# Reordering the rotation sums and the recurrence gates of a one-core, three-layer transformer kernel

## The chip, the core and the metric

The kernel runs on one core of a Trainium2 chip. The metric is the device time of one execution in microseconds (us). The kernel before takes 1228.55 us, the median of three runs (1228.42 to 1229.12).

## The reference

The input is a sequence of 256 tokens of width 1024, in float32. Two layers of a first block and one layer of a second block follow one another. Cut to what matters here:

```python
# first block, layer 1 ("odd"): dilated attention; 3 groups x (q, k, v) x 16 heads of 64
hcat = (rms_norm(x, g) @ w_in).reshape(b, s, 3, 3, 16, 64)
q = apply_rope(hcat[:, :, :, 0], cos, sin)     # x1*c - x2*s | x2*c + x1*s
k = apply_rope(hcat[:, :, :, 1], cos, sin)
v = hcat[:, :, :, 2]
x = x + dilated_attention(q, k, v) @ w_o
x = x + square(relu(rms_norm(x) @ w1)) @ w2    # both layers end in this MLP

# second block
proj = rms_norm(x, g) @ w_in_2                 # 7 parts: xa, ga, qm, km, vm, qx, gate logits
xa = causal_dwconv(xa, conv_w, conv_b)         # 4 taps, 512 channels
r = sigmoid(xa @ w_a + b_a); i = sigmoid(xa @ w_x + b_x)   # per head, 8 heads of 64
log_a = -8 * r * softplus(-lam)
u = sqrt(-expm1(2 * log_a)) * i * xa
h_t = exp(log_a)_t * h_(t-1) + u_t             # recurrence over the tokens
y_a = h * gelu(ga)
# then block attention, cross-attention, three gated branches, a gated MLP with a convolution
```

## The kernel before, in words

Every weight matrix is cut into 192 slabs of up to 1 MB, which the program uses strictly in order. A slab goes through the same steps each time. SyncE (SP) loads it into one of five buffers `raw`. ScalarE (ACT) rounds it to a reduced float format, `whi` (three buffers, `high`, line 1118). VectorE (DVE), or in some stages GpSimd (POOL), subtracts the two to get the rest, `wlo` (five buffers, `low`, line 1558). TensorE (PE) multiplies `whi` and `wlo` with the activations, which are split in the same way into `XH` and `XL`. Three products are added up in PSUM: high by high, high by low, low by high. The code calls the step that makes slab n+2 ready `ahead(n)`.

The order of the work on each engine is written by hand: five functions (`tensor`, `scalar`, `vector`, `gpsimd`, `sync`) issue each engine's instructions in program order, and named events tie them together. An engine that waits for an event holds up all that stands behind it on that engine.

A slab whose products are feature-major is computed by one of two functions. `features` (through `product`, line 536) goes chunk by chunk: high weight, low weight, high weight, so its second matmul already needs `wlo`. `features_low_last` (line 550) first does all 32 matmuls that use `whi`, then the 16 that use `wlo`. Both issue 48 matmuls of 256 columns. `tokens` and `by_tokens` are token-major.

**The odd stage** has the slabs 50 to 85, and i counts them from 0. The first ten (`EARLY`) come before the attention steps start; i = 0 to 5 are q and k slabs, 6 to 8 are v slabs, 9 is again q. A q or k slab is rotated as follows. ACT copies the product from PSUM into `TA` (line 1376), and its queue starts four DMAs that write the halves swapped into `TB` (line 1382). POOL multiplies `TB` by the sine (line 2339; the event `sine`). DVE multiplies the PSUM product by the cosine (line 1939) and later adds `TB` (line 1918, function `rotate`; the event `rotated`). ACT may copy slab k only when slab k-2 has been added. In the first ten slabs `rotate` runs one slab behind: the sum of slab k stands on DVE behind `ahead` of slab k+2 and ahead of that slab's cosine product.

**The in2 stage** has the slabs 122 to 133, and n counts them from 0. DVE scales each product (line 2014) and runs one of four causal convolutions (`conv(0)` to `conv(3)`, lines 2039 and 2043) at n = 1 to 4. On PE, `lru_gate` (line 994) multiplies the convolved chunks 0 to 3 by the small gate matrices; it is issued twice, behind n = 6 and n = 7. Its chunk c waits for `conv(c)`. ACT takes the sigmoid (line 1413), then a tanh (line 1437) at n = 8 and an exponential (line 1442) at n = 9; DVE forms a ratio in two parts (lines 2056 to 2060) at n = 9 and 10; ACT takes a root (line 1446) at n = 11; then comes the recurrence (line 2073) during the first attention steps.

Of the kernel before, what the change touches and what calls it, by code (L numbers as in the profile page):

```python
# [7 lines left out]
ALU = mybir.AluOpType  # L8
# [71 lines left out]
class Tally:  # L80
# [9 lines left out]
    def tell(self, sem, *events, by=1):  # L90
        n = self.count[sem.name] = self.count.get(sem.name, 0) + by
        for event in events:
            if self.rehearsing:
                assert event not in self.value, event
                self.value[event] = sem, n
            assert self.value[event] == (sem, n), event
        return sem, by

    def at(self, event):
        return self.value.get(event, (None, 0)) if self.rehearsing else self.value[event]  # L100
# [117 lines left out]
DILATED = dilated_slabs()  # L218

EARLY = 10  # L220
# [74 lines left out]
def build(nc, A, out):  # L295
    with ExitStack() as ctx:
# [216 lines left out]
        def tensor(pe):  # L513
            once = Once(pe)
# [434 lines left out]
            def odd_slab(i):  # L949
                n, (kind, hb, g, k) = SLAB_ODD + i, DILATED[i]  # L950
                if i == 0:
                    features_by_chunks([n, n + 1], x, lambda: last_rows_back(0))
                    sums("n2", 1, cols=True, dilated=True)
                elif kind == "qk":
                    if i > 1:
                        (features_low_last if i < 6 else features)(n, x)
                elif kind == "v":
                    tokens(n, x)
                else:
                    for t in range(2):  # L960
                        if k == 0:
                            bank(("odd v", hb, g, t))
                        b = ps[bank_of.get(("odd v", hb, g, t), 0)]
                        event = ("product", "odd v", hb, g, t) if k else ("weights", n) if t else None
                        xt = [(h[:, t * P:t * P + P], l[:, t * P:t * P + P], mh, ml) for h, l, mh, ml in x[4 * k:4 * k + 4]]
                        product(b[:, :], xt, w_ready(n, 4, 0, 512), event, first=k == 0, last=k == 1)
                    released[n] = [event]
# [17 lines left out]
            def lru_gate(n):  # L985
                for j in range(2):
                    b = bank(("lru", n, j))
                    once.wait_ge(*at("lruw"))
                    for m in range(2):
                        c = 2 * j + m  # L990
                        once.wait_ge(*at(("conv", c)))
                        for a in range(2):
                            p = slice(64 * a, 64 * a + 64)
                            mm = pe.matmul(b[p, m * S:(m + 1) * S], wab[p, n, c, :], XC[p, c, :], start=True, stop=True)  # L994
                    mm.then_inc(*tell(s_product, ("product", "lru", n, j)))
# [11 lines left out]
            for n in range(12):  # L1007
                if n == 0:
                    features_by_chunks([IN2, IN2 + 1], x, lambda: last_rows_back(1))
                elif n == 1:  # L1010
                    pass
                elif n in (6, 7):
                    by_tokens("in2 values", IN2 + n, n - 6)
                else:
                    (features_low_last if n < 6 else features)(IN2 + n, x)
                if n == 0:
                    sums("n4", 1, cols=True)
                    sums("n5", 0, cols=True)
                if n in (6, 7):
                    lru_gate(n - 6)  # L1020

            def gate(j):
                by_tokens(("gate", j // 2), BLENDS + BLEND.index(("gate", j)), j % 2)
# [81 lines left out]
        def scalar(act):  # L1105
# [301 lines left out]
            def lru_gate(n):  # L1407
                dst, bl = ((AR, "ba"), (UI, "bx"))[n]
                for j in range(2):
                    b = take(("lru", n, j))  # L1410
                    for m in range(2):
                        c = 2 * j + m
                        i = act.activation(dst[:, c, :], b[:, m * S:(m + 1) * S], ACT.Sigmoid, bias=gain(bl, c))
                    i.then_inc(*tell(s_act_out, ("taken", "lru", n, j)))
# [6 lines left out]
            for n in range(12):  # L1421
                if n != 1:
                    ahead(IN2 + n)
                if n == 0:
                    root("n4", 1, cols=True)
                    ahead(IN2 + 1)
                    once.wait_ge(*at("both mean"))
                    act.activation(RS[:, 0, 0:S + 2], RS[:, 0, 0:S + 2], ACT.Sqrt).then_inc(*tell(s_root, "both sqrt"))
                if n == 7:
                    by_tokens("in2 values", lambda t: VB[:, t, :])  # L1430
                if n in (6, 7):
                    lru_gate(n - 6)
                if n == 8:
                    once.wait_ge(*at("rate"))
                    for c in range(4):
                        once.wait_ge(*at(("taken", "lru", 1, 1)))
                        m = act.activation(UM[:, c, :], AR[:, c, :], ACT.Tanh, scale=L[6][:, c:c + 1])
                    m.then_inc(*tell(s_act, "lru tanh"))
                if n == 9:
                    once.wait_ge(*at("lru tanh"))  # L1440
                    for c in range(4):
                        m = act.activation(AR[:, c, :], AR[:, c, :], ACT.Exp, scale=L[7][:, c:c + 1])
                    m.then_inc(*tell(s_act, "lru a"))
                if n == 11:
                    once.wait_ge(*at("lru ratio"))
                    act.activation(UM, UM, ACT.Sqrt, scale=2.0).then_inc(*tell(s_act, "lru root"))
# [103 lines left out]
        def vector(dve):  # L1550
# [355 lines left out]
                *tell(s_sum, ("norm", "n2")))  # L1906


            rotated, pending = [0], []

            def rotate(behind):

                while len(pending) > behind:
                    hb, g, w, k = pending.pop(0)
                    dst = QKV[hb % 3][3 * g + w]
                    once.wait_ge(*at(("sine", k)))
                    once.wait_ge(*at(("taken", "slab", SLAB_ODD + DILATED.index(("qk", hb, g, w)))))
                    dve.tensor_tensor(dst, dst, TB[k % 2][:, :], ALU.add).then_inc(*tell(s_dve, ("odd", hb, g, w), ("rotated", k)))

            def odd_slab(i):  # L1920
                n, (kind, hb, g, w) = SLAB_ODD + i, DILATED[i]
                if i != 1:
                    ahead(n)
                if kind != "qk":
                    rotate(0)
                    return
                rotate(1)
                if i == 0:
                    mean("n2", 1, 8, cols=True)
                    ahead(n + 1)  # L1930
                    inverse("n2", 1, cols=True)
                    once.wait_ge(*at("dmask"))
                    once.wait_ge(*at(WIDE["odd"]))
                    for k in range(2):
                        m = dve.tensor_tensor(RP[:, k * S:k * S + S], ropef[:, k * S:k * S + S], RS[:, 1, 0:S], ALU.mult)
                    m.then_inc(*tell(s_dve, "rp"))
                    once.wait_ge(*at("rp"))
                b = take(("slab", n), [("copied", n)])
                dve.tensor_tensor(pair(QKV[hb % 3][3 * g + w]), pair(b[:, :]), twice(RP[:, 0:S]), ALU.mult).then_inc(
                    *tell(s_dve_out, ("taken", "slab", n)))  # L1940
                if i >= EARLY:
                    rotate(0)
                pending.append((hb, g, w, rotated[0]))
                rotated[0] += 1

            for i in range(EARLY):
# [129 lines left out]
            for n in range(12):  # L2076
                if n == 0:
                    ahead(IN2)
                    factors()
                if n < 4:  # L2080
                    j = n % 2
                    scaled(IN2 + n, (XA if n < 2 else GA)[:, 2 * j:2 * j + 2, :])
                elif n not in (6, 7):
                    dst, by, j = {4: (QB, 0.125, 0), 5: (KB, 1.0, 0), 8: (QX, 128.0 ** -0.5, 0), 9: (QB, 0.125, 1),
                                  10: (KB, 1.0, 1), 11: (QX, 128.0 ** -0.5, 1)}[n]
                    scaled(IN2 + n, dst[:, 2 * j:2 * j + 2, :], by)
                if n:
                    ahead(IN2 + n + 1)
                if 1 <= n < 5:
                    conv(n - 1)  # L2090
                if n in (6, 7):
                    restart(4 * (n - 6))
                if n in (9, 10):
                    lru_ratio(n - 9)

            def gate(j):
                ahead(BLENDS + BLEND.index(("gate", j)))
# [404 lines left out]
```

## Time and profile before

| | |
|---|---|
| median of three runs | 1228.55 us |
| the profiled execution: its own time | 1228.55 us |
| the profiled execution: its span, first to last instruction | 1226.7 us |
| PE / PE weight loads / DVE / ACT / POOL busy | 1216.7 / 1117.0 / 799.4 / 630.7 / 206.3 us |
| mean granted TensorE clock | 1.000 of full speed |

Matmuls overlap in the pipeline, so a row's duration is its latency and the distance between two starts is what a matmul costs: 0.12 us for 256 columns. PE counts as idle only when nothing is in flight, so a pause shorter than the overlap, about 0.16 us, does not show in the idle figures. Instructions of one line and kind that follow one another without a pause are merged into one row with a count.

### The profile page before, as it was taken

What the parts mean: (1) busy time and instruction counts of PE and PEld (TensorE: products, weight loads), DVE (VectorE), ACT (ScalarE), POOL (GpSimd) and SP (SyncE); (2) the same over time, 40 slices, a digit from 0 to 9 for tenths busy, and PEclk for the clock granted to TensorE, in tenths of its full rate; (3) what the DMA queues carried; (4) which work ended last, traced back from release to release, by engine and by line L of the source; (5) the groups of instructions that cost most, each with busy time, mean ns of one, the idle gap of its engine ahead of it and who ended that gap; (6) DMA issues with size and microseconds to landing.
All of it is one profiled execution on the core that took longest, in us unless ns stands there. A gap on an engine that the chain in (4) does not pass through costs nothing.

```text
span 1226.7 us, 20617 instructions
## 1 busy us (share of the span) xinstructions
PE 1216.7 (99%) x8673; PEld 1117.0 (91%) x8673; DVE 799.4 (65%) x1071; ACT 630.7 (51%) x785; POOL 206.3 (17%) x160
## 2 busy tenths in 40 slices
PE   9999999999999999999999999999999999999998
PEld 8988999988899989999999988898878899999986
DVE  7878666644475765676876754587875577656643
ACT  5574455544455454445655544456576645444342
POOL 2500010000011201210310000010010695443100
PEclk9999999999999999999999999999999999999999
DMA  8733456555676555654355555555554455555551
GB/s 246 250 99 109 137 179 192 179 198 179 206 226 204 174 179 176 189 177 147 104 166 178 179 199 194 183 187 165 179 169 141 157 189 185 174 172 180 199 181 60
DMA packets 162076, 214.33 MB, mean 175 GB/s; under 512 B 5259, under 2 KB 117198, under 8 KB 161982
## 3 DMA queue, kind: packets, MB, share of 16 engines
q1 hardware_dynamic: 156574, 205.11, 51.8%
q10 hardware_dynamic: 5216, 7.42, 2.1%
q8 instruction: 69, 1.13, 0.4%
q0 software_dynamic: 192, 0.46, 0.2%
q14 instruction: 25, 0.20, 0.0%
HBM read 205.63 MB, written 1.05 MB: 168 GB/s over the span
## 4 chain that ended last, share of the span: by engine, by line
PE 91%; DVE 4%; ACT 2%; issue 1%; DMA 1%; SPq 0%; ACTq 0%; DVEq 0%
PE ps L536 74%; PE ps L550 4%; PE ps L608 3%; PE ps L705 3%; PE ps L742 2%; PE ps L713 2%; DVE wlo L1558 1%; DMA raw<-in_ev_w_in_dram 1%; ACT whi L1118 1%; DVE XT L1691 0%; ACT SN L1180 0%; PE ps L994 0%; PE ps L629 0%; DVE XL L1596 0%; PE ps L796 0%
## 5 line engine op out<-in xcount | busy, mean ns | idle before, releaser
L1558 DVE TENSOR_TENSOR wlo<-raw,whi 128x2048 fp32r<-128x2048 f32 (+1 forms) x167 | 385.8, 2312 | 223.1 <-ACT whi L1118 222.9
L1118 ACT ACTIVATE whi<-raw 128x2048 fp32r<-128x2048 f32 x188 | 357.8, 1906 | 199.9 <-PE ps L536 179.8
L536 PE MATMUL ps<-XH,whi 128*128 128x256 f32 x1224 | 341.8, 285 | 0.0
L536 PE MATMUL ps<-XH,wlo 128*128 128x256 f32 x1224 | 339.6, 283 | 0.3 <-DVE wlo L1558 0.2
L536 PE MATMUL ps<-XL,whi 128*128 128x256 f32 x1224 | 339.4, 283 | 0.0
L536 PEld LDWEIGHTS ps<-XH,wlo 128*128 128x128 f32 x1224 | 231.7, 192 | 0.7 <-DVE wlo L1558 0.7
L536 PEld LDWEIGHTS ps<-XH,whi 128*128 128x128 f32 x1224 | 231.7, 192 | 0.6 <-issue 0.4
L536 PEld LDWEIGHTS ps<-XL,whi 128*128 128x128 f32 x1224 | 231.6, 192 | 0.0
L536 PE MATMUL ps<-whi,HL 128*128 128x512 f32 (+1 forms) x416 | 148.7, 373 | 0.0
L536 PE MATMUL ps<-whi,HH 128*128 128x512 f32 x384 | 147.2, 390 | 0.0
L536 PE MATMUL ps<-wlo,HH 128*128 128x512 f32 x368 | 143.2, 389 | 0.0
L2273 POOL TENSOR_TENSOR wlo<-raw,whi 128x512 fp32r<-128x512 f32 x88 | 115.3, 1345 | 142.3 <-ACT whi L1118 142.2
L536 PE MATMUL ps<-whi,XH 128*128 128x512 f32 (+1 forms) x288 | 98.1, 348 | 0.0
L2339 POOL TENSOR_TENSOR TB<-TB,BIG 128x512 f32<-128x512 f32 x24 | 37.0, 1543 | 362.3 <-DMA TB<-TA 362.3
L536 PE MATMUL ps<-wlo,XH 128*128 128x512 f32 (+1 forms) x288 | 96.4, 343 | 0.0
L536 PE MATMUL ps<-whi,XL 128*128 128x512 f32 (+1 forms) x288 | 96.3, 342 | 0.0
L536 PEld LDWEIGHTS ps<-whi,HL 128*128 128x128 f32 x416 | 76.0, 188 | 13.6
L1180 ACT ACTIVATE SN<-SN,stat 128x512 f32<-128x512 f32 (+2 forms) x64 | 38.2, 597 | 95.9 <-DVE stat L1630 93.3
L536 PEld LDWEIGHTS ps<-whi,HH 128*128 128x128 f32 x384 | 71.9, 188 | 14.8
L536 PEld LDWEIGHTS ps<-wlo,HH 128*128 128x128 f32 x368 | 69.1, 188 | 14.4
L536 PEld LDWEIGHTS ps<-whi,XH 128*128 128x128 f32 x288 | 53.6, 190 | 6.5 <-issue 0.7
L536 PEld LDWEIGHTS ps<-wlo,XH 128*128 128x128 f32 x288 | 53.6, 189 | 6.5
(271 smaller groups left out, 1790.4 us busy)
## 6 DMA issues: line engine op xcount, KB each, us to landing
raw<-in_mlp_w_dram SPq DMA_DIRECT2D x64, 1024.0 KB, 5.3
raw<-in_od_w_in_dram SPq DMA_DIRECT2D x36, 1024.0 KB, 5.4
raw<-in_w_in_dram SPq DMA_DIRECT2D x24, 1024.0 KB, 5.1
raw<-in_w_ffn_gate_dram SPq DMA_DIRECT2D x12, 1024.0 KB, 5.2
raw<-in_w_ffn_up_dram SPq DMA_DIRECT2D x12, 1024.0 KB, 5.2
raw<-in_w_ffn_down_dram SPq DMA_DIRECT2D x12, 1024.0 KB, 5.0
TB<-TA ACTq DMA_DIRECT2D x96, 64.0 KB, 4.1
raw<-in_w_branch_dram SPq DMA_DIRECT2D x6, 1024.0 KB, 5.0
```

What stands on the lines that cost most here:

```text
L536: m = pe.matmul(to, l[c][a], r[c][b], start=first and k == 0, stop=last and k == 3 * n - 1)
L550: i = pe.matmul(b[:, m * S:m * S + S], w[m][c][a], x[c][z], start=m == c == a == z == 0, stop=m == a == 1 and c == len(x) - 1)
L608: i = pe.matmul(b[n][:, m * S:m * S + S], h[a], x[c][z], start=m == c == a == z == 0, stop=m == 1 and c == 7 and z == 1)
L705: m = pe.matmul(banks[u][:, lo:hi], l, r, start=start, stop=stop)
L713: m = pe.transpose(b[:, to:to + P], SN[:, u % 3, of:of + P], ident[:, :])
L742: m = pe.matmul(b[p0:p0 + n, a:z], v, PT[:, u % 3, lo:hi], start=start, stop=stop)
L1118: act.activation(whi_of(n), raw_of(n), ACT.Copy, scale=1.0).then_inc(*tell(s_whi, ("whi", n)))
L1180: m = act.activation(SN[:, u % 3, lo:hi], src[:, lo:hi], ACT.Exp, bias=stat[:, u % 3, k:k + 1], scale=-1.0 if biased else 1.0, accum_out=s ...
L1558: dve.tensor_tensor(wlo_of(n), raw_of(n), f32(whi_of(n)), ALU.subtract).then_inc(*tell(s_wlo, ("wlo", n)))
L2273: m = pool.tensor_tensor(lo[:, v], r[:, v], f32(hi[:, v]), ALU.subtract)
L2339: pool.tensor_tensor(z, z, twice(RP[:, S:512]), ALU.mult).then_inc(*tell(s_pool, ("sine", k)))
```

## The change

Four things are changed. First, slabs 54 and 55 (i = 4 and 5) are computed by `features`, no longer by `features_low_last`. Second, DVE's `rotate` of a slab stands directly behind the cosine product of the next q or k slab, in the first ten slabs as in the later ones. Third, PE issues `lru_gate` behind n = 5 and n = 6, and ACT's sigmoids move with it. Fourth, ACT's tanh and exponential stand at n = 7 and 8, and DVE's ratio at n = 8 and 9.

```diff
@@ tensor, odd_slab
-                        (features_low_last if i < 6 else features)(n, x)
+                        (features_low_last if i < 4 else features)(n, x)
@@ tensor, in2 loop
-                if n in (6, 7):
-                    lru_gate(n - 6)
+                if n in (5, 6):
+                    lru_gate(n - 5)
@@ scalar, in2 loop
-                if n in (6, 7):
-                    lru_gate(n - 6)
-                if n == 8:
+                if n in (5, 6):
+                    lru_gate(n - 5)
+                if n == 7:
                     once.wait_ge(*at("rate"))
...
-                if n == 9:
+                if n == 8:
                     once.wait_ge(*at("lru tanh"))
@@ vector, odd_slab
-            def rotate(behind):
-                while len(pending) > behind:
-                    hb, g, w, k = pending.pop(0)
+            def rotate():
+                if pending[0] is None:
+                    return
+                hb, g, w, k = pending[0]
+                pending[0] = None
...
                 if kind != "qk":
-                    rotate(0)
+                    rotate()
                     return
-                rotate(1)
...
                 dve.tensor_tensor(pair(QKV[hb % 3][3 * g + w]), pair(b[:, :]), twice(RP[:, 0:S]), ALU.mult).then_inc(
                     *tell(s_dve_out, ("taken", "slab", n)))
-                if i >= EARLY:
-                    rotate(0)
-                pending.append((hb, g, w, rotated[0]))
+                rotate()
+                pending[0] = hb, g, w, rotated[0]
@@ vector, in2 loop
-                if n in (9, 10):
-                    lru_ratio(n - 9)
+                if n in (8, 9):
+                    lru_ratio(n - 8)
```

On DVE at the start of the odd stage, before (L1939 is the cosine product of slab 51, then of 52 and 53; L1558 makes `wlo` of slabs 54, 55 and 56; L1918 adds the sine part of slabs 50, 51 and 52):

```order
L1939 TENSOR_TENSOR BIG<-ps,BIG 128x512 [waits s_act_out]
L1558 TENSOR_TENSOR wlo<-raw,whi 128x2048 [waits s_whi,s_raw4]
L1918 TENSOR_TENSOR BIG<-BIG,TB 128x512 [waits s_dve_out,s_pool]
L1939 TENSOR_TENSOR BIG<-ps,BIG 128x512 [waits s_act_out,s_product]
L1558 TENSOR_TENSOR wlo<-raw,whi 128x2048 [waits s_whi,s_raw0]
L1918 TENSOR_TENSOR BIG<-BIG,TB 128x512 [waits s_dve_out,s_pool]
L1939 TENSOR_TENSOR BIG<-ps,BIG 128x512 [waits s_act_out,s_product]
```

The same place now (L1940 and L1920 are the old L1939 and L1918):

```order
L1940 TENSOR_TENSOR BIG<-ps,BIG 128x512 [waits s_act_out]
L1920 TENSOR_TENSOR BIG<-BIG,TB 128x512 [waits s_dve_out,s_pool]
L1558 TENSOR_TENSOR wlo<-raw,whi 128x2048 [waits s_whi,s_raw4]
L1940 TENSOR_TENSOR BIG<-ps,BIG 128x512 [waits s_act_out,s_product]
L1920 TENSOR_TENSOR BIG<-BIG,TB 128x512 [waits s_dve_out,s_pool]
L1558 TENSOR_TENSOR wlo<-raw,whi 128x2048 [waits s_whi,s_raw0]
```

The sum of slab 50, with its wait for POOL, now stands ahead of the `wlo` of slab 54.

On PE, the change from slab 53 to slab 54, before:

```order
L550 MATMUL ps<-XH,wlo 128x256 [waits s_wlo]
L550 MATMUL ps<-XH,wlo 128x256 x15
L550 MATMUL ps<-XH,whi 128x256 [waits s_whi,s_dve_out]
L550 MATMUL ps<-XL,whi 128x256
```

and now:

```order
L550 MATMUL ps<-XH,wlo 128x256 [waits s_wlo]
L550 MATMUL ps<-XH,wlo 128x256 x15
L536 MATMUL ps<-XH,whi 128x256 [waits s_whi,s_dve_out]
L536 MATMUL ps<-XH,wlo 128x256 [waits s_wlo]
```

Slab 54's wait for `wlo` has moved from its 33rd matmul to its second.

On PE in the in2 stage, now (L550 ends slab 127, which is n = 5; L994 is the first gate, a wait for each chunk's convolution; L536 begins slab 128):

```order
L550 MATMUL ps<-XH,wlo 128x256 [waits s_wlo]
L550 MATMUL ps<-XH,wlo 128x256 x15
L994 MATMUL ps<-BIG,SN 64x256 [waits s_dve,s_lruw]
L994 MATMUL ps<-BIG,SN 64x256
L994 MATMUL ps<-BIG,SN 64x256 [waits s_dve]
L994 MATMUL ps<-BIG,SN 64x256
L994 MATMUL ps<-BIG,SN 64x256 [waits s_dve]
L994 MATMUL ps<-BIG,SN 64x256
L994 MATMUL ps<-BIG,SN 64x256 [waits s_dve]
L994 MATMUL ps<-BIG,SN 64x256
L536 MATMUL ps<-whi,XH 128x512 [waits s_whi]
```

Before, the first gate stood behind the 24 matmuls of slab 128; now it stands ahead of them. In the trace each of these eight L994 rows shows as two instructions.

## Rows read from the trace of the kernel before

**Rows 1.** The page: busy time, and the clock in 40 slices.

```profile
PE 1216.7 (99%) x8673; PEld 1117.0 (91%) x8673; DVE 799.4 (65%) x1071; ACT 630.7 (51%) x785; POOL 206.3 (17%) x160
...
PEclk9999999999999999999999999999999999999999
```

**Rows 2.** Waits of PE: engine, line, whom for; us in total, times, longest.

```profile
PE ps L574 <- ACT whi L1247: 1.2, 2, 0.8
PE ps L830 <- DVE ones L1741: 1.0, 1, 1.0
PE ps L713 <- DVE SN L1645: 0.6, 1, 0.6
PE ps L608 <- DVE XL L1596: 0.5, 1, 0.5
PE ps L742 <- DVE PT L1653: 0.2, 1, 0.2
PE ps L536 <- DVE wlo L1558: 0.2, 1, 0.2
```

**Rows 3.** Timeline of PE, slab 54: start, duration, instruction, count.

```profile
357.53 0.28 PE L550 MATMUL ps<-XH,whi 128*128 128x256 f32 x1
357.65 0.28 PE L550 MATMUL ps<-XL,whi 128*128 128x256 f32 x1
...
361.37 2.08 PE L550 MATMUL ps<-XH,wlo 128*128 128x256 f32 x16
363.29 0.28 PE L550 MATMUL ps<-XH,whi 128*128 128x256 f32 x1
```

**Rows 4.** Timeline of DVE, slabs 50 to 55; in brackets idle time before it.

```profile
351.92 1.29 DVE L1939 TENSOR_TENSOR BIG<-ps,BIG 128x512 f32<-128x512 f32 x2
354.33 2.29 DVE L1558 TENSOR_TENSOR wlo<-raw,whi 128x2048 fp32r<-128x2048 f32 x1 [1.13 <-ACT whi L1118]
357.81 0.69 DVE L1918 TENSOR_TENSOR BIG<-BIG,TB 128x512 f32<-128x512 f32 x1 [1.19 <-POOL TB L2339]
359.30 0.69 DVE L1939 TENSOR_TENSOR BIG<-ps,BIG 128x512 f32<-128x512 f32 x1 [0.79 <-ACT TA L1376]
361.10 2.29 DVE L1558 TENSOR_TENSOR wlo<-raw,whi 128x2048 fp32r<-128x2048 f32 x1 [1.11 <-ACT whi L1118]
363.31 0.68 DVE L1918 TENSOR_TENSOR BIG<-BIG,TB 128x512 f32<-128x512 f32 x1
```

**Rows 5.** Timeline of POOL, the sine products of slabs 50 and 51.

```profile
355.80 1.98 POOL L2339 TENSOR_TENSOR TB<-TB,BIG 128x512 f32<-128x512 f32 x1 [194.33 <-DMA TB<-TA]
359.90 1.29 POOL L2339 TENSOR_TENSOR TB<-TB,BIG 128x512 f32<-128x512 f32 x1 [2.12 <-DMA TB<-TA]
```

**Rows 6.** Timeline of ACT, the swaps of slab 50 and the copy of slab 52.

```profile
349.27 2.52 ACTq L1382 DMA_DIRECT2D TB<-TA  x4
...
358.60 0.60 ACT L1376 ACTIVATE TA<-ps 128x512 f32<-128x512 f32 x1 [4.37 <-DVE BIG L1918]
359.09 1.91 ACT L1118 ACTIVATE whi<-raw 128x2048 fp32r<-128x2048 f32 x1
```

**Rows 7.** Timeline of PE, where it waited for a `wlo` at 628 us.

```profile
628.06 0.38 PE L536 MATMUL ps<-XH,wlo 128*128 128x256 f32 x1 [0.18 <-DVE wlo L1558]
```

**Rows 8.** Timeline of DVE, that `wlo`.

```profile
625.57 2.44 DVE L1558 TENSOR_TENSOR wlo<-raw,whi 128x2048 fp32r<-128x2048 f32 x1 [1.77 <-ACT whi L1118]
```

**Rows 9.** Timeline of PE, slab 128 and the first gate.

```profile
833.83 0.40 PE L536 MATMUL ps<-whi,XH 128*128 128x512 f32 x1
...
839.39 1.94 PE L994 MATMUL ps<-BIG,SN 64*64 64x256 f32 x16
841.26 0.50 PE L536 MATMUL ps<-whi,XH 128*128 128x512 f32 x1
```

**Rows 10.** Timeline of DVE, n = 4: scaling, `wlo`, and the last convolution.

```profile
834.13 0.68 DVE L2014 SCALAR_TENSOR_TENSOR BIG<-ps,RS 128x512 f32<-128x512 f32 x1
834.73 2.28 DVE L1558 TENSOR_TENSOR wlo<-raw,whi 128x2048 fp32r<-128x2048 f32 x1
836.93 0.41 DVE L2039 TENSOR_SCALAR BIG<-BIG,V 128x256 f32<-128x256 f32 x1
837.37 1.52 DVE L2043 SCALAR_TENSOR_TENSOR BIG<-BIG,V 128x255 f32<-128x255 f32 x3
```

**Rows 11.** Timeline of ACT, the root.

```profile
876.71 1.06 ACT L1446 ACTIVATE BIG<-BIG 128x1024 f32<-128x1024 f32 x1 [7.07 <-DVE BIG L2060]
```

**Rows 12.** Timeline of PE, the same eight score matmuls at two attention steps.

```profile
889.51 0.93 PE L705 MATMUL ps<-BIG 64*128 64x128 f32 x8
890.37 0.55 PE L713 MATMUL ps<-ident,SN 128*128 128x128 f32 x3
...
902.14 0.93 PE L705 MATMUL ps<-BIG 64*128 64x128 f32 x8
903.27 0.33 PE L742 MATMUL ps<-PT,BIG 128*64 128x128 f32 x2 [0.21 <-DVE PT L1653]
```

More of the change, by code:

```diff
@@ L1906, in vector @@
                 *tell(s_sum, ("norm", "n2")))
-            rotated, pending = [0], []
-            def rotate(behind):
-                while len(pending) > behind:
-                    hb, g, w, k = pending.pop(0)
[L1915 to L1918, printed above, removed]
+            rotated, pending = [0], [None]
+            def rotate():
[3 more added lines that the diff above has]
+                pending[0] = None
+                dst = QKV[hb % 3][3 * g + w]
+                once.wait_ge(*at(("sine", k)))
+                once.wait_ge(*at(("taken", "slab", SLAB_ODD + DILATED.index(("qk", hb, g, w)))))
+                dve.tensor_tensor(dst, dst, TB[k % 2][:, :], ALU.add).then_inc(*tell(s_dve, ("odd", hb, g, w), ("rotated", k)))
             def odd_slab(i):
```

## The prediction

> **What bounds the kernel now.** I read the busy line first. PE is busy 1216.7 of 1226.7 us and its clock stands at the full level (2.4 GHz) in every slice [rows 1]. The waits view then says what PE ever waited for: 3.7 us in seven waits, 1.2 of them at L574 and 1.0 at L830, in the start-up [rows 2]. So the kernel is one uninterrupted stream of matmuls. An edit that moves work on ACT, DVE or POOL can win no more than the rest of those waits, and any new wait on PE goes to the end of the kernel in full, since nothing behind it has slack to give back. The change adds and removes no arithmetic: the matmuls are as many and as wide, and rows of the line-550 kind start 0.12 us apart as those of line 536 do elsewhere (357.53, 357.65) [rows 3]. The question at each place is whether the operand is there when PE, unstalled, comes to it. The timelines of PE and DVE at the two places, side by side, answer that.
>
> **Part 1: slab 54.** Before, PE starts slab 54 at 357.53 and comes to its first low matmul at 361.37 [rows 3]. Its `wlo` is made at 354.33 to 356.62, and only then does DVE wait for the sine of slab 50 [rows 4]. Now that wait stands ahead of the `wlo`, and PE wants the `wlo` at its second matmul, at 357.65. Step by step:
>
> - The sine of slab 50 starts when the swaps have landed, at 355.80 [rows 5]; the last swap was issued by 351.79 [rows 6]. The change moves none of this.
> - It took 1.98 us, the next one 1.29 [rows 5]. The long one started while DVE was in the middle of the `wlo` (354.33 + 2.29 = 356.62, 0.82 later), and the excess is 0.69. I read this as POOL having waited for DVE. Now DVE stands idle there, so I take 1.30: sine ready at 357.10.
> - The sum follows 0.03 later (357.78 to 357.81) and lasts 0.69 [rows 4, 5]: 357.13 to 357.82.
> - A DVE row that follows at once starts 0.08 before the recorded end of the one before (361.10 + 2.29 against 363.31) [rows 4]. So the `wlo` of slab 54 runs from 357.74 to 360.03.
> - PE started 0.05 after the `wlo` it once waited for (625.57 + 2.44 = 628.01; 628.06) [rows 7, 8]: 360.08.
>
> The stall is 360.08 - 357.65 = **2.43 us**. If the sine were as long as before, it would be 357.81 + 0.69 - 0.08 + 2.29 + 0.05 - 357.65 = 3.11, the upper end. The lower end is a swap that lands sooner. The next sine started at 359.90, 2.1 us after POOL was free, so landing times do vary; if slab 50's came 1.3 us sooner the stall would be 1.1. I take 2.43, because nothing ahead of 355.80 changes.
>
> The Trainium skill (SBUF — State Buffer, "Who interferes with whom") says that a DVE instruction with two SBUF inputs and a GpSimd instruction that reads SBUF exclude each other for the whole instruction. By that rule the sum is the 2.43 above; without it, 3.11. The trace agrees with the rule, by the 1.98 against 1.29.
>
> Does slab 55, now `features` too, stall again? ACT copies slab 52 0.09 after the sum, at 357.9 where it was 358.60 [rows 6], so the `whi` of slab 55 is ready near 360.3. DVE does the cosine of 52 behind the `wlo` of 54 (to 360.7), waits for the sine of 51 (359.90, or behind the `wlo` at 360.03, plus 1.29: 361.3), adds to 362.0, and makes the `wlo` of 55 by 364.3. PE comes to slab 55 at 363.29 + 2.43 = 365.7. That is 1.4 us in time: no second stall, and only because of the first. For slab 56, POOL gets to the sine of 52 behind that `wlo` at 364.3, the sum ends at 366.3, and the `wlo` of 56 at 368.5, where PE comes to it 5.76 after 365.7, at 371.5: 3 us in time, and each later slab has more.
>
> **Part 2: the first gate.** Before, the gate starts at 839.39; `conv(3)` ended at 837.37 + 1.52 = 838.89, half a microsecond ahead [rows 9, 10]. Now the gate stands where slab 128 started, at 833.83 [rows 9]. Its 16 instructions are 1.87/16 = 0.117 us apart [rows 9]; the twelve of chunks 0 to 2 go through, and chunk 3 is wanted at 833.83 + 12 x 0.117 = 835.23. DVE's order up to `conv(3)` is unchanged and it runs without a pause through that stretch [rows 10], so it can't be earlier. PE starts chunk 3 at 838.89 + 0.05 = 838.94. The stall is **3.71 us**. It could be smaller only if DVE's queue were shorter, which no edit does; bounds 3.6 to 3.9 by the latency of a wait (0.0 to 0.15). Queued behind on PE is slab 128, whose operands have long been there, so nothing hides in the wait. ACT holds the `whi` of slab 130 behind this gate's sigmoids: they end near 840.6, the `whi` 1.9 later at 842.5, and PE wants it at about 853 (slab 128, a gate and slab 129 later).
>
> **What is won.** The chain sigmoid, tanh, exponential, ratio, root is about one slab earlier against PE. ACT's 7.07 us idle before the root [rows 11] shrinks. PE gets from this only what it waited for behind the chain. The same eight score matmuls take 890.37 - 889.51 = 0.86 us undisturbed and 903.27 - 902.14 = 1.13 where the probabilities came late: 0.27 us [rows 12]. I take it as won (bounds 0 and 0.27). The 0.6 us wait at L713 [rows 2] lies in the attention steps of the odd stage, where the order is unchanged; I take 0, bound a gain of 0.6.
>
> **Sum.** 2.43 + 3.71 - 0.27 = +5.87 us. The profiled execution has its own time of 1228.55, 1.85 over its span and equal to the median of the runs. Forecast: **1234.4 us**, 0.48% slower. Its own range, from the bounds: 1228.55 + 1.1 + 3.6 - 0.9 = 1232.4 to 1228.55 + 3.1 + 3.9 = 1235.6.
>
> **Rivals.**
>
> *The clock falls (8%).* The longest wait of PE in the rows is 1.0 us and the clock never left the full level [rows 1, 2]. No row shows what 3.7 us of silence do. If the grant fell to 1.2 GHz, matmuls would be 0.24 us apart for a while, and every microsecond's worth of work would take two. If half of slab 128 (833.83 to 839.39, 5.56 us) ran so, that adds 2.8: 1237.2; all of it, 5.6: 1240.0. The Trainium skill (TensorE: Matmul & The Clock Gate, "HAM oscillation") says that gaps in which the array idles can drop the clock. No row here shows it.
>
> *Only one stall is real (7%).* Slab 54 alone gives 1228.55 + 2.4 = 1231.0, the gate alone 1228.55 + 3.7 - 0.3 = 1232.0. For it: each rests on one chain of waits that I followed. Against: in both the instruction that must end first is in plain sight and starts too late even if all latencies are nil.
>
> *Not slower (7%): the earlier releases are what counts.* ACT waited 4.37 us for a rotation sum [rows 6] and 7.07 us for the ratio [rows 11]; both go earlier. If PE's waits at L713 and L742 came from those and no new one arose, the time would be 1228.55 - 0.6 - 0.3 = 1227.7, within the noise. It decides at two points: `wlo` of slab 54 done by 357.65 and `conv(3)` by 835.23. The rows put them at 360.0 and 838.9. A gain over 0.2% is out of reach altogether: it would take 2.5 us, and outside the start-up PE waited 1.5.
>
> **How the numbers follow.** The forecast holds 78%. 0.2% (2.5 us, about what a measurement of this kernel can tell from no change) puts the border at 1231.0. The forecast, the clock case and most of the one-stall case are slower: 91%. The not-slower case and a little of the one-stall case are the same: 7%. Faster: 2%, for what I may have overlooked. The range takes in the forecast's own, the gate-alone case at the bottom and the first half of the clock case at the top: 1231.5 to 1237.0.
>
> **What would show it.** In the profile of the changed kernel the waits of PE should have two new entries: L536 for DVE's `wlo` of about 2.3 us once, near 360, and L994 for DVE's L2043 of about 3.6 us once, near 841 (the stage comes 2.4 us later). The sine at 355.80 should last 1.3 us. The wait at L742 for DVE's L1653 should be gone. DVE's `wlo` of slab 54 should end near 360.0. The granted clock should read 1.00 throughout. I am wrong if either new wait is missing, or if the clock dips.

## The result

The changed kernel takes 1237.58 us, the median of four runs (1234.70 to 1238.38); the kernel before took 1228.84 beside it. The ratio is 1.0065, with a 95% interval of 1.0048 to 1.0083; it is formed from all executions and not from the two medians, which would give 1.0071. The kernel became slower by two thirds of a percent, 3.2 us more than forecast by the median.

The profiled execution took 1235.95 us, its span is 1234.0, and the mean granted clock is 0.997 where it was 1.000. The busy times are those of before within 2 us:

```profile
PE 1218.7 (99%) x8673; PEld 1118.9 (91%) x8673; DVE 800.3 (65%) x1071; ACT 631.4 (51%) x785; POOL 206.5 (17%) x160
```

The waits of PE, in the form of [rows 2] (in us: total, times, longest):

```profile
PE ps L994 <- DVE BIG L2043: 3.5, 1, 3.5
PE ps L536 <- DVE wlo L1558: 2.2, 1, 2.2
PE ps L830 <- DVE ones L1741: 1.0, 1, 1.0
PE ps L574 <- ACT whi L1247: 0.8, 2, 0.4
PE ps L713 <- DVE SN L1645: 0.6, 1, 0.6
PE ps L608 <- DVE XL L1596: 0.4, 1, 0.4
PE ps L629 <- DVE SQ L1774: 0.3, 1, 0.3
PE ps L536 <- DVE OL L1663: 0.2, 1, 0.2
```

Two long waits are new, for the two instructions that the prediction named. The wait at L742 is no longer in the list. The small ones, most of them in the start-up, differ by some tenths from execution to execution.

**Slab 54.** The timelines of POOL, DVE and PE, one fence each, answer to [rows 5], [rows 4] and [rows 3]:

```profile
355.84 1.29 POOL L2339 TENSOR_TENSOR TB<-TB,BIG 128x512 f32<-128x512 f32 x1 [194.25 <-DMA TB<-TA]
```

```profile
357.17 0.69 DVE L1920 TENSOR_TENSOR BIG<-BIG,TB 128x512 f32<-128x512 f32 x1 [3.86 <-POOL TB L2339]
357.77 2.29 DVE L1558 TENSOR_TENSOR wlo<-raw,whi 128x2048 fp32r<-128x2048 f32 x1
359.98 0.68 DVE L1940 TENSOR_TENSOR BIG<-ps,BIG 128x512 f32<-128x512 f32 x1
```

```profile
357.63 0.28 PE L536 MATMUL ps<-XH,whi 128*128 128x256 f32 x1
360.12 0.58 PE L536 MATMUL ps<-XH,wlo 128*128 128x256 f32 x1 [2.21 <-DVE wlo L1558]
360.49 0.42 PE L536 MATMUL ps<-XL,whi 128*128 128x256 f32 x1
360.71 0.42 PE L536 MATMUL ps<-XH,whi 128*128 128x256 f32 x1
360.93 0.41 PE L536 MATMUL ps<-XH,wlo 128*128 128x256 f32 x1
```

The sine lasts 1.29 us, since DVE no longer holds it up; the sum follows, then the `wlo`, and PE's second matmul starts at 360.12 where 357.75 was due: 2.37 us. The last three rows show something more. The matmuls are 0.22 us apart and no longer 0.12; over the thirteen distances from 360.49 to 363.27 the mean is 0.214.

**The gate**, on PE and DVE, as in [rows 9] and [rows 10]:

```profile
837.79 1.51 PE L994 MATMUL ps<-BIG,SN 64*64 64x256 f32 x12
842.82 0.65 PE L994 MATMUL ps<-BIG,SN 64*64 64x256 f32 x4 [3.52 <-DVE BIG L2043]
```

```profile
838.61 2.28 DVE L1558 TENSOR_TENSOR wlo<-raw,whi 128x2048 fp32r<-128x2048 f32 x1
840.80 0.41 DVE L2039 TENSOR_SCALAR BIG<-BIG,V 128x256 f32<-128x256 f32 x1
841.25 1.52 DVE L2043 SCALAR_TENSOR_TENSOR BIG<-BIG,V 128x255 f32<-128x255 f32 x3
```

Twelve instructions go through, and the last four start 0.05 after `conv(3)`'s end at 842.77. They were due at 837.79 + 12 x 0.117 = 839.19: 3.63 us.

**The clock.** The view by stretches, of the changed kernel (columns: stretch and its length; busy time and count of PE, its weight loads, DVE, ACT, POOL; granted clock; DMA share and GB/s):

```profile
358.00:359.80 1.80, 0.00 (x0) 0.00 (x0) 1.80 (x1) 1.80 (x2) 0.00 (x0) 1.00 0.50 115
360.00:363.00 3.00, 2.88 (x13) 2.89 (x14) 2.10 (x4) 1.00 (x3) 1.28 (x1) 0.50 0.99 327
363.40:366.00 2.60, 2.60 (x24) 2.60 (x23) 1.66 (x2) 1.35 (x1) 0.41 (x1) 1.00 0.37 95
838.00:842.80 4.80, 1.30 (x12) 0.56 (x8) 4.69 (x8) 0.84 (x2) 0.00 (x0) 1.00 0.67 218
843.00:847.00 4.00, 4.00 (x20) 2.98 (x19) 1.10 (x2) 2.64 (x3) 0.00 (x0) 1.00 0.00 0
```

PE is silent from 358 on, and as it takes up work the grant stands at 0.50, the lower level of 1.2 GHz, for 3 us and more. I call such a stretch a fall. In the same execution the longer silence at the gate brought none. Matmuls 0.214 us apart that would be 0.12 apart lose 0.094 each; thirteen of them, from 360.49 to 363.27, make 1.2 us, and the first distance behind the wait is 0.37, 0.25 more than 0.12: 1.5 together. The profiled execution closes: 2.37 + 3.63 + 1.5 - 0.27 = 7.2, and the span grew by 1234.0 - 1226.7 = 7.3.

The timed executions fit. The one with clock 0.999 took 1234.70, about what was forecast. Three with 0.996 took 1237.55, 1237.61 and 1238.38, some 3 us more: two falls of 1.5, or one long one, as a later experiment has it. Where their falls lie was not recorded. The mean clock is a rough sign only. It takes in the end of the execution, behind PE's last matmul, where the grant drops as well (0.76 from 1225.00 to 1226.70 in the kernel before), so executions of the kernel before mostly read 0.998 to 1.000.

### The profile page after: what moved, and what is told of

Same layout as the page of the kernel before. It is cut to its first block, busy times and chain, and to the rows that moved or that the text cites. A ratio compares the mean times of both kernels' runs of the same rounds, so it can differ in the third digit from the quotient of the medians.

```text
span 1234.0 us, 20616 instructions
## 1 busy us (share of the span) xinstructions
PE 1218.7 (99%) x8673; PEld 1118.9 (91%) x8673; DVE 800.3 (65%) x1071; ACT 631.4 (51%) x785; POOL 206.5 (17%) x160
## 4 chain that ended last, share of the span: by engine, by line
PE 89%; DVE 6%; ACT 2%; DMA 1%; issue 1%; SPq 0%; ACTq 0%; POOL 0%; DVEq 0%
PE ps L536 77%; PE ps L705 3%; PE ps L608 3%; PE ps L742 2%; PE ps L713 2%; DVE wlo L1558 2%; DMA raw<-in_ev_w_in_dram 1%; ACT whi L1118 1%; DVE XT L1691 0%; DVE XL L1596 0%; DVE BIG L2043 0%; DMA TB<-TA 0%; ACTq L1382 0%; DVE RS L1591 0%; PE ps L878 0%
## 5 line engine op out<-in xcount | busy, mean ns | idle before, releaser
L1558 DVE TENSOR_TENSOR wlo<-raw,whi 128x2048 fp32r<-128x2048 f32 (+1 forms) x167 | 385.8, 2311 | 224.2 <-ACT whi L1118 224.0
L536 PE MATMUL ps<-XH,wlo 128*128 128x256 f32 x1256 | 349.5, 284 | 2.4 <-DVE wlo L1558 2.2
L536 PE MATMUL ps<-XH,whi 128*128 128x256 f32 x1256 | 351.3, 285 | 0.0
L536 PE MATMUL ps<-XL,whi 128*128 128x256 f32 x1256 | 349.2, 283 | 0.0
L536 PEld LDWEIGHTS ps<-XH,wlo 128*128 128x128 f32 x1256 | 238.6, 192 | 3.1 <-DVE wlo L1558 3.1
L536 PEld LDWEIGHTS ps<-XH,whi 128*128 128x128 f32 x1256 | 238.6, 192 | 0.2
L536 PEld LDWEIGHTS ps<-XL,whi 128*128 128x128 f32 x1256 | 238.5, 192 | 0.0
L536 PE MATMUL ps<-whi,HL 128*128 128x512 f32 (+1 forms) x416 | 148.7, 373 | 0.0
L536 PE MATMUL ps<-whi,HH 128*128 128x512 f32 x384 | 147.2, 390 | 0.0
L536 PE MATMUL ps<-wlo,HH 128*128 128x512 f32 x368 | 143.2, 389 | 0.0
L536 PE MATMUL ps<-whi,XH 128*128 128x512 f32 (+1 forms) x288 | 98.2, 349 | 0.0
L536 PE MATMUL ps<-wlo,XH 128*128 128x512 f32 (+1 forms) x288 | 96.4, 343 | 0.0
L536 PE MATMUL ps<-whi,XL 128*128 128x512 f32 (+1 forms) x288 | 96.3, 342 | 0.0
L536 PEld LDWEIGHTS ps<-whi,HL 128*128 128x128 f32 x416 | 76.0, 188 | 13.5
L536 PEld LDWEIGHTS ps<-whi,HH 128*128 128x128 f32 x384 | 71.9, 188 | 14.7
L536 PEld LDWEIGHTS ps<-wlo,HH 128*128 128x128 f32 x368 | 69.1, 188 | 14.5
L536 PEld LDWEIGHTS ps<-whi,XH 128*128 128x128 f32 x288 | 53.6, 190 | 6.9 <-issue 1.1
L536 PEld LDWEIGHTS ps<-wlo,XH 128*128 128x128 f32 x288 | 53.6, 189 | 6.5
```

The lines of the kernel that those rows point to most:

```text
L536: m = pe.matmul(to, l[c][a], r[c][b], start=first and k == 0, stop=last and k == 3 * n - 1)
L1558: dve.tensor_tensor(wlo_of(n), raw_of(n), f32(whi_of(n)), ALU.subtract).then_inc(*tell(s_wlo, ("wlo", n)))
```

## The experiments

Each kernel was timed beside the kernel before on the same chip. All ratios are to that.

| kernel | median us | ratio | 95% interval | longest new PE waits |
|---|---|---|---|---|
| slab 54 part | 1231.39 | 1.0025 | 1.0014 to 1.0036 | 2.3 |
| gate part | 1233.42 | 1.0043 | 1.0030 to 1.0055 | 3.5 |
| rotate alone | 1227.66 | 0.9997 | 0.9988 to 1.0006 | 0.6 |
| features alone | 1228.59 | 1.0003 | 0.9994 to 1.0012 | 0.2 |
| chain alone | 1228.51 | 1.0000 | 0.9991 to 1.0008 | none |
| all but features | 1234.30 | 1.0047 | 1.0034 to 1.0059 | 3.5 |
| convolutions earlier | 1233.30 | 1.0035 | 1.0023 to 1.0048 | 2.2, 0.8 |
| filled | 1233.76 | 1.0042 | 1.0028 to 1.0056 | 0.5 |
| changed, again | 1237.25 | 1.0069 | 1.0056 to 1.0081 | 2.2, 3.5 |
| filled, again | 1234.34 | 1.0048 | 1.0034 to 1.0062 | 1.0, 0.5 |
| slab 54 filled only | 1237.25 | 1.0068 | 1.0055 to 1.0080 | 3.5 |
| rotate and chain | 1228.22 | 0.9996 | 0.9987 to 1.0005 | none |

### Which edit costs what

**The slab 54 part alone**: the two edits of the odd stage, on the kernel before.

```diff
-                        (features_low_last if i < 6 else features)(n, x)
+                        (features_low_last if i < 4 else features)(n, x)
...
-                rotate(1)
...
-                if i >= EARLY:
-                    rotate(0)
-                pending.append((hb, g, w, rotated[0]))
+                rotate()
+                pending[0] = hb, g, w, rotated[0]
```

> Only the odd stage's edits (rotate behind the cosine product, slabs 54 and 55 by features); gates and chain as before. My theory: PE waits 2.2 to 2.4 us for the wlo of slab 54, and the clock falls to half for one stretch of 3.4 us in many executions, which costs 1.6 more: 1231.2 without a fall, 1232.8 with one. Rival (the clock falls only after the longer wait at the gate): 1231.2 in every execution, clock at its full level.

Measured 1231.39 (1230.77 to 1232.41), ratio 1.0025: 3.1 us. PE's wait was 2.3 us and the profiled execution had a fall, in this stretch:

```profile
360.00:363.00 3.00, 3.00 (x16) 3.00 (x16) 2.26 (x2) 1.47 (x2) 0.71 (x1) 0.50 0.81 251
```

The rival that the clock falls only at the longer wait is out. But 3.1 us leaves only 0.7 above a wait of 2.4, by my estimate less than half a fall on average, and the seven mean clocks, 0.997 to 0.999, hardly differ from those of the kernel before. With this part alone most executions seem to have had none.

**The gate part alone**: the edits of the in2 stage, on the kernel before.

```diff
-                if n in (6, 7):
-                    lru_gate(n - 6)
+                if n in (5, 6):
+                    lru_gate(n - 5)
# on PE and ACT; and tanh n == 7, exp n == 8, lru_ratio(n - 8) at n in (8, 9)
```

> Only the in2 stage's edits (gates one slab earlier on PE and ACT; tanh, exponential and ratio one slab earlier). My theory: PE waits 3.5 us at L994 for conv(3), 0.3 won at L742: 1232.2 without a fall of the clock, 1233.8 with one. Rival (the in2 edits are harmless and the whole loss is slab 54's): 1228.5. Rival (the clock does not fall here, since in the profiled execution of the changed kernel it fell only near slab 54): 1232.2 in every execution.

Measured 1233.42 (1232.52 to 1233.94), ratio 1.0043: 5.3 us. One fall in the profiled execution, at the gate. The stretches of silence, fall and recovery, and then the 512-column matmuls of slab 128 on PE:

```profile
835.00:838.00 3.00, 0.00 (x0) 0.00 (x0) 2.89 (x5) 0.18 (x1) 0.00 (x0) 1.00 0.91 311
839.30:842.50 3.20, 3.20 (x9) 2.46 (x8) 0.83 (x1) 2.27 (x3) 0.00 (x0) 0.50 0.00 0
843.00:846.00 3.00, 3.00 (x14) 2.25 (x12) 0.96 (x1) 0.00 (x0) 0.00 (x0) 1.00 0.00 0
```

```profile
839.96 0.63 PE L536 MATMUL ps<-whi,XH 128*128 128x512 f32 x1
840.39 0.63 PE L536 MATMUL ps<-whi,XL 128*128 128x512 f32 x1
840.82 0.63 PE L536 MATMUL ps<-wlo,XH 128*128 128x512 f32 x1
```

They are 0.43 us apart where 0.23 is usual. Both of its rivals are out: the in2 edits are not harmless, and the clock falls there too. The parts' excesses, 0.25 and 0.43%, add up to 0.68 where the whole has 0.65, the same within the intervals.

**Rotate alone** and **features alone** part the first pair further. The diffs are the two halves of the first one above.

> Only the move of rotate; slabs 54 and 55 still by features_low_last. My theory: the wlo of slab 54 ends near 360.0 and PE wants it at 361.4, so no wait: 1228.6, within 0.1% of the kernel before. Rival (the move by itself delays DVE enough to stall PE): 1230.5 or more.

Measured 1227.66 (1227.27 to 1230.15), ratio 0.9997.

> Only slabs 54 and 55 by features, rotate as before. My theory: the wlo of slab 54 ends at 356.6, ahead of 357.65, and that of slab 55 at 363.4, just when PE wants it: 1228.6. Rival (features is slower in itself, or slab 55 stalls): 1230 or more, with a wait at L536 for L1558 near 363.5.

Measured 1228.59 (1227.62 to 1229.85), ratio 1.0003. Neither costs anything that the timing can tell (it would see some 0.1%): the wait at slab 54 needs both, a later `wlo` and an earlier need for it. Both kernels show how narrow it is, for each has a small wait of its own. In features alone PE waited for slab 55, and the matmul starts 0.47 us behind the one before it:

```profile
362.68 0.39 PE L536 MATMUL ps<-XH,wlo 128*128 128x256 f32 x1 [0.19 <-DVE wlo L1558]
```

In rotate alone it waited 0.64 for slab 56, whose `wlo` stood behind a sine that started at 365.84, late by its swaps:

```profile
370.12 0.39 PE L536 MATMUL ps<-wlo,XH 128*128 128x256 f32 x1 [0.64 <-DVE wlo L1558]
```

**The chain alone**: ACT and DVE's part of the in2 edits, the gates left where they were.

```diff
-                if n == 8:                       # tanh
+                if n == 7:
-                if n == 9:                       # exp
+                if n == 8:
-                if n in (9, 10):
-                    lru_ratio(n - 9)
+                if n in (8, 9):
+                    lru_ratio(n - 8)
```

> Only tanh, exponential and ratio one slab earlier on ACT and DVE; the gates stay behind slabs 128 and 129. My theory: no wait is added, the 0.3 us before L742 goes: 1228.3. Rival (the chain needs the gates one slab earlier too, and stalls ACT and then PE): 1229.5 or more.

Measured 1228.51 (1227.59 to 1230.62), ratio 1.0000. The wait at L742 is gone from the list, and 0.3 us is under what this comparison resolves. The gate part's loss is the gates'.

**All but features**: the changed kernel with one edit undone.

```diff
-                        (features_low_last if i < 4 else features)(n, x)
+                        (features_low_last if i < 6 else features)(n, x)
```

> The changed kernel with slabs 54 and 55 by features_low_last again. My theory: the wait at slab 54 goes and that at the gate stays: as the gate part alone, 1232.2 to 1233.8. Rival (the moved rotate is what costs, whichever function follows): 1235 or more.

Measured 1234.30 (1233.19 to 1235.62), ratio 1.0047, as the gate part alone within the intervals; the median is 0.5 above what I expected. The profiled execution had longer waits than usual in the start-up (1.6 us at L574 and 1.3 at L629), which none of the edits touches, and one fall, at the gate. The wait at slab 54 is gone, so it is the pair that costs.

**Convolutions earlier**: on the changed kernel.

```diff
-                if 1 <= n < 5:
-                    conv(n - 1)
+                if n < 4:
+                    conv(n)
```

> The changed kernel with DVE's four convolutions at n = 0 to 3 instead of 1 to 4. My theory: conv(3) then ends 2.7 us earlier, the wait at L994 is 1.0 instead of 3.7 us, and with it one of two falls of the clock goes: 1233.5 to 1235. Rival (the gate waits for something else, such as its weights): no difference from the changed kernel.

Measured 1233.30 (1231.26 to 1234.05), ratio 1.0035, just under the expected span. The wait at the gate followed the convolution:

```profile
PE ps L536 <- DVE wlo L1558: 2.2, 1, 2.2
PE ps L830 <- DVE ones L1741: 1.0, 1, 1.0
PE ps L994 <- DVE BIG L2043: 0.8, 1, 0.8
```

Moved ahead by one slab, the convolution took 2.7 us off the wait: L994 waited for `conv(3)` and nothing else. The profiled execution, 1231.26, had no fall at all, after 2.2 us of waiting at slab 54.

### Is the rest the clock?

**Filled**: the changed kernel, with matmuls in place of the silence, whose results the real ones overwrite.

```diff
                 b = bank(("slab", n))
+                if n == SLAB_ODD + 4:
+                    ...
+                    for _ in range(20):
+                        pe.matmul(b[:, 0:S], w[0], xh, start=True, stop=True)
...
+                        if n == 0 and c == 3:
+                            for _ in range(7):
+                                for a in range(2):
+                                    p = slice(64 * a, 64 * a + 64)
+                                    pe.matmul(b[p, S:2 * S], wab[p, n, 2, :], XC[p, 2, :], start=True, stop=True)
                         once.wait_ge(*at(("conv", c)))
```

> The changed kernel with matmuls that only fill time: 20 of 256 columns ahead of slab 54's first matmul (2.4 us), and 14 of the gate's own kind (3.3 us) ahead of the gate's last chunk; their results are overwritten. My theory (the loss above 5.9 us is the clock, which falls when PE is silent): both stretches are filled, the clock stays at its full level, and the kernel takes 1234.5, about 3 less than the changed kernel without them although it does more. Rival (the clock has no part in it): 1237.5 or more.

Measured 1233.76 (1233.56 to 1234.46). The changed kernel was not timed in that comparison, so I ran both again on one chip.

> The changed kernel, run beside the next three on one chip. My theory (two waits of 2.2 and 3.5 us, and up to two falls of the clock at 1.7 us each): 1.0048 to 1.0075 of the kernel before, median near 1.0065, with granted clocks from 0.999 (no fall) to 0.996 (two).

Measured 1237.25 (1234.88 to 1238.45), ratio 1.0069. The profiled execution had a fall at each wait:

```profile
359.50:362.70 3.20, 3.06 (x14) 3.06 (x15) 2.53 (x4) 1.43 (x3) 1.28 (x1) 0.50 0.99 320
...
844.20:847.40 3.20, 3.20 (x9) 2.45 (x8) 1.53 (x1) 1.57 (x1) 0.00 (x0) 0.50 0.00 0
```

> The changed kernel with both waits filled by matmuls whose results are overwritten. My theory: no fall, 1.0045, 2 to 3 us below the changed kernel on the same chip. Rival (the clock has no part and the earlier difference was that of two chips): the same as the changed kernel.

Measured 1234.34 (1234.01 to 1235.36), ratio 1.0048, and in its profiled execution the clock kept its level in both places:

```profile
358.00:363.00 5.00, 5.00 (x43) 4.99 (x43) 4.14 (x5) 2.66 (x3) 1.30 (x1) 1.00 0.74 241
835.00:845.00 10.00, 9.50 (x70) 6.60 (x69) 6.90 (x11) 3.48 (x5) 0.00 (x0) 1.00 0.33 108
```

(The wait of 1.0 in the table lies in the first 100 us, not at slab 54.) The kernel does more and its median is 2.9 us lower. The samples are small and the intervals of the two ratios just overlap, but only the fastest execution without the filling, 1234.88, lies among the filled ones, and the first filling, on another chip, gave 1233.56 to 1234.46. This is the step that shows the clock. What is left, 5.6 us over the kernel before, is the two waits themselves.

**Slab 54 filled only**: the first hunk of the diff above without the second.

> Only the wait at slab 54 is filled. My theory: falls are left at the gate alone, so the time lies between the other two: 1.0050 to 1.0060, clock 0.999 or 0.997. Rival (falls come only at slab 54): as filled on both sides, 1.0045.

Measured 1237.25 (1235.89 to 1237.85), ratio 1.0068. This missed: it is no faster than the changed kernel. The profiled execution had no fall at slab 54, but at the gate it had one twice as long:

```profile
836.00:839.90 3.90, 1.38 (x12) 0.62 (x10) 3.83 (x6) 0.84 (x2) 0.00 (x0) 1.00 0.72 240
840.00:843.00 3.00, 2.10 (x7) 1.16 (x8) 1.41 (x3) 0.94 (x3) 0.00 (x0) 0.50 0.07 25
843.00:846.70 3.70, 3.70 (x10) 2.93 (x9) 1.90 (x1) 1.70 (x1) 0.00 (x0) 0.50 0.00 0
```

Three profiles show what such a fall costs, by the time from the gate's last instructions to the start of slab 129. The changed kernel has no fall there (its last four gate instructions start at 842.82, above), the gate part has one, and slab 54 filled only has the long one (its L1000 is L994):

```profile
850.96 0.50 PE L536 MATMUL ps<-whi,XH 128*128 128x512 f32 x1
```

```profile
838.24 0.65 PE L994 MATMUL ps<-BIG,SN 64*64 64x256 f32 x4 [3.52 <-DVE BIG L2043]
...
847.98 0.50 PE L536 MATMUL ps<-whi,XH 128*128 128x512 f32 x1
```

```profile
840.90 1.12 PE L1000 MATMUL ps<-BIG,SN 64*64 64x256 f32 x4 [3.52 <-DVE BIG L2049]
...
851.74 0.50 PE L536 MATMUL ps<-whi,XH 128*128 128x512 f32 x1
```

That is 8.14, 9.74 and 10.84 us: the fall costs 1.6 and the long one 2.7. The gate part's 1233.42 and the 2.4 us of filling would make 1235.8; the executions lie 0 to 2 above that. Long falls would account for about 1.1 of it, but I have the position and length of a fall only where there was a profile. So how much the filling of slab 54 gives by itself is not shown. What decides whether a fall is short or long stays open.

**Rotate and chain**: the moves that cost nothing, on the kernel before.

```diff
-                if n in (9, 10):
-                    lru_ratio(n - 9)
+                if n in (8, 9):
+                    lru_ratio(n - 8)
# with tanh at n == 7, exp at n == 8, and rotate() behind the cosine product
```

> The kernel before with the moves that cost nothing: rotate behind the cosine product, and tanh, exponential and ratio one slab earlier; slabs 54 and 55 and the gates as before. My theory: 0.9993 to 1.0000 of the kernel before, at most 0.9 us faster, which the interval will hardly tell from no change. Rival (the edits need each other): slower than 1.0010.

Measured 1228.22 (1226.98 to 1229.81), ratio 0.9996. It is no slower, and whether it is faster can't be told. Waits at L713 and L742 are both absent. Only the second is the edits' doing: the wait at L713 is also missing in chain alone, which leaves the odd stage as it was, and is there in the changed kernel, which has the moved `rotate`.

```profile
PE ps L574 <- ACT whi L1247: 1.2, 2, 0.9
PE ps L830 <- DVE ones L1741: 1.0, 1, 1.0
PE ps L608 <- DVE XL L1596: 0.4, 1, 0.4
```

With 2.6 us of waits left in the list, the order of the other engines has at most that to give.

## Why the prediction was right, and where it fell short

**What bounds it: right.** PE is a stream without slack, and each wait came through to the end in full. The span of the profiled execution closes to a tenth, though the small waits of the start-up alone move by more than that between executions.

**Slab 54: right**, 2.43 forecast and 2.37 measured. The sine started at 355.84, as before at 355.80, but now with DVE standing idle, and came out at 1.29, not 1.98. So the reading that POOL had been waiting for DVE held, and with it the Trainium skill's rule of exclusive use (SBUF — State Buffer, "Who interferes with whom"). Slab 55 did not stall. Rotate alone and features alone show the cause by experiment: only together do they cost.

**The gate: right**, 3.71 forecast and 3.63 measured; the earlier convolutions show its cause.

**What is won: right in kind.** The same eight score matmuls now take 910.62 - 909.76 = 0.86 at the second step, as at the first:

```profile
909.76 0.93 PE L705 MATMUL ps<-BIG 64*128 64x128 f32 x8
910.62 0.88 PE L742 MATMUL ps<-PT,BIG 128*64 128x128 f32 x12
```

ACT's idle before the root shrank from 7.07 us [rows 11] to 2.55:

```profile
879.82 1.06 ACT L1446 ACTIVATE BIG<-BIG 128x1024 f32<-128x1024 f32 x1 [2.55 <-DVE BIG L2060]
```

No timing can tell the 0.27 from nothing.

**The clock: the step that failed.** I gave a fall 8%, behind the gate's wait alone, since the longest wait of before, 1.0 us, had none, and put it at nothing in the sum. That wait proves little, for it is the one ahead of PE's first matmul; between matmuls the longest was 0.8 us:

```profile
1.04 3.85 PE L830 MATMUL ps<-ones 128*128 128x128 f32 x20 [1.04 <-DVE ones L1741]
```

In fact most executions of the changed kernel have falls, by their times and mean clocks, 2.2 us of waiting can be enough for one, and there are two places. By the prediction's own sign ("or if the clock dips") it was wrong here. The median, 1237.58, is the clock case, 0.6 above the top of my range; the ratio of 1.0065 on 1228.55 makes 1236.5, inside it. That it comes so close to the top is in part luck: the price was wrong the other way. I put 2.8 to 5.6 on one fall, and a fall costs 1.5 to 1.6, the long one 2.7, so that two falls came to what I had priced one at. One reason is that I let the distances double, 0.12 to 0.24, where 0.214 was measured; the other is that the lower level lasted some 3 us, where half of slab 128 at half speed would have been 5.6. The terms of the sum were right to a tenth, and the likeliest case still was not the one that occurred, because I treated a term of 1.5 to 3.2 us as an accident.

**The single-stall and not-slower rivals: out.** Each part alone is slower, with intervals clear of 1.

## What to carry to other kernels

When one engine is busy 99% of the time, lay its timeline beside that of the engine it reads from and compare, for each moved instruction, the time it is due and the time its operand is ready. Two moves that are all but free one by one can cost together, when one makes an operand later and the other asks for it earlier; an order that reads its late operand last (as `features_low_last` does) is cover, and is given up only where nothing ahead of that operand has moved. On TensorE, count a new wait of the lengths seen here, 2.2 us and 3.5, at its own length plus some 1.5 us for matmuls that may then run at the lower clock.

## What the runs showed of the hardware

A silence of PE of 2.2 or 2.3 us was followed in three of four profiles (the changed kernel, its repeat, the slab 54 part) by a stretch at 1.2 GHz, and in one (convolutions earlier, span 1229.3, clock 1.000) by none. After the 3.5 us at the gate, four profiles had a fall and one, the changed kernel's first, had none. Shorter waits between matmuls, 0.8 us in the kernel before and 1.3 in the start-up of all but features, brought none. The granted clock came back while PE worked on, at 363.4 us in the changed kernel. In a stretch at the lower level 256-column matmuls start 0.21 us apart against 0.12, and 512-column ones 0.43 against 0.23. The Trainium skill (TensorE: Matmul & The Clock Gate, "HAM oscillation — how this bites in real kernels") has the effect, and these runs agree with it that idle gaps bring the clock down.

A POOL product of two SBUF operands that started 0.82 us before the end of a DVE subtraction of two SBUF operands took 1.98 us [rows 5]; with DVE idle, in the changed kernel, the same product took 1.29. It was longer by 0.69, most of what was left of the subtraction.
